# Two 2 MB weight loads of a decoder layer, each cut along the partitions into 120 and 8

## The reference

```python
def peer_ffn(x, w_query, sub_keys, expert_u, expert_v):
    q = (xt @ w_query).reshape(T, PEER_HEADS, 2, PEER_KEY_DIM // 2)
    s = jnp.einsum('thcd,hckd->thck', q, sub_keys)
    s_top, i_top = lax.top_k(s, PEER_TOPK)
    ...                                   # 16 of 256 candidates a head: e_idx, g
    def block(args):
        xb, eb, gb = args
        u = expert_u[eb]
        h = gelu(einsum('td,thkd->thk', xb, u))
        v = expert_v[eb]
        return einsum('thk,thkd->td', gb * h, v)
    ...
```

## Time and profile before

| | |
|---|---|
| median of three runs | 970.4 us (968.57 to 971.49) |
| profiled execution: its own time | 969.14 us |
| its span, first to last instruction | 967.3 us |
| busy: PE / DVE / ACT / POOL | 79% / 61% / 44% / 31% of the span |
| moved by DMA | 335.28 MB, of it 268.45 MB by the gathers (q0) and 66.12 MB by SP (q1) |
| DMA rate from slice 11 of 40 on | 402 to 423 GB/s in each slice but the last |
| chain of waits, by engine | DMA 45%, PE 36%, ACT 8%, DVE 7% |

### The profile page before, as it was taken

How to read it: one execution, slowest core, us unless ns; L and a number is a source line. 1 busy time by engine, 2 the same in 40 slices (tenths; PEclk the granted TensorE clock), 3 DMA queues, 4 the chain that set the end, 5 groups by cost and what they waited for, 6 DMA issues and landing times.

```text
span 967.3 us, 11099 instructions
## 1 busy us (share of the span) xinstructions
PE 766.8 (79%) x3718; PEld 329.6 (34%) x3722; DVE 589.3 (61%) x1409; ACT 428.4 (44%) x1186; POOL 299.7 (31%) x294
## 2 busy tenths in 40 slices
PE   7999999999787999979695757676866666666665
PEld 6876754574443444434131212121211111111010
DVE  1615340453579878877567647587666766767545
ACT  1144212552348967964343424254543434434333
POOL 0010021000325543535333344344443344343320
PEclk9999999999968997979886778597876766677765
DMA  7633233726599999999999999999999999999992
GB/s 262 250 118 121 101 140 142 303 89 249 223 421 421 420 422 405 402 421 420 423 422 421 421 423 421 418 422 421 420 420 421 421 421 421 421 420 421 422 420 110
DMA packets 45353, 335.28 MB, mean 347 GB/s; under 512 B 6000, under 2 KB 6000, under 8 KB 8560
## 3 DMA queue, kind: packets, MB, share of 16 engines
q0 software_dynamic: 36864, 268.45, 67.0%
q1 hardware_dynamic: 8432, 66.12, 17.5%
HBM read 333.50 MB, written 1.05 MB: 346 GB/s over the span
## 4 chain that ended last, share of the span: by engine, by line
DMA 45%; PE 36%; ACT 8%; DVE 7%; issue 3%; POOL 1%; DVEq 0%; SPq 0%; POOLq 0%; ACTq 0%
DMA late<-in_uv,eidx 32%; DMA ring<-in_uv,eidx 11%; PE ps L691 9%; PE ps L1027 7%; PE ps L683 6%; ACT late L1075 4%; ACT L1075 3%; PE ps L815 3%; PE ps L850 3%; DVE late L1731 2%; PE ps L959 1%; DMA wring<-in_wts 1%; DVE ring L1731 1%; ACT tmp L1075 1%; POOL late L1825 1%
## 5 line engine op out<-in xcount | busy, mean ns | idle before, releaser
L1075 ACT ACTIVATE late<-late 128x1 f32<-128x1 f32 (+3 forms) x787 | 221.9, 285 | 345.1 <-DVE late L1731 325.5
L1027 PE MATMUL ps<-ring,late 64*64 64x512 f32 x928 | 161.0, 779 | 95.7 <-ACT late L1075 95.5
L1027 PE MATMUL ps<-late 64*64 64x512 f32 x960 | 169.9, 799 | 65.3 <-ACT late L1075 65.2
L1825 POOL DMA_INDIRECT late<-in_uv,eidx x120 | 134.3, 1119 | 242.4 <-PE ps L1027 177.0
L1731 DVE CUSTOM_DVE_ANT_0 late<-late,x_sb 128x1024 f32<-128x1024 f32 x120 | 146.9, 1225 | 99.2 <-DMA late<-in_uv,eidx 98.6
L1731 DVE CUSTOM_DVE_ANT_0 ring<-ring,x_sb 128x1024 f32<-128x1024 f32 x116 | 142.1, 1225 | 87.2 <-DMA ring<-in_uv,eidx 86.7
L1825 POOL DMA_INDIRECT ring<-in_uv,eidx x116 | 126.8, 1093 | 189.4 <-PE ps L1027 180.8
L1075 ACT ACT_TABLE_LOAD x80 | 102.6, 1283 | 13.3 <-PE ps L683 11.9
L1027 PEld LDWEIGHTS ps<-ring,late 64*64 64x64 f32 x928 | 29.2, 154 | 195.6 <-ACT late L1075 181.4
L1027 PEld LDWEIGHTS ps<-late 64*64 64x64 f32 x960 | 32.1, 161 | 172.3 <-ACT late L1075 154.1
L691 PE MATMUL ps<-wring,tmp 128*128 128x347 f32 (+4 forms) x256 | 85.4, 492 | 0.0
(11 more groups left out here) (235 smaller groups left out, 745.2 us busy)
## 6 DMA issues: line engine op xcount, KB each, us to landing
wring<-in_wts SPq DMA_DIRECT2D x22, 2048.0 KB, 8.7
wring<-in_wts SPq DMA_DIRECT2D x2, 1428.0 KB, 5.8
wring<-in_wts SPq DMA_DIRECT2D x2, 1388.0 KB, 6.3
lnw<-in_ln SPq DMA_DIRECT2D x4, 512.0 KB, 12.5
late<-in_uv,eidx POOLq DMA_INDIRECT x120, 17.5
ring<-in_uv,eidx POOLq DMA_INDIRECT x116, 17.8
wring<-in_wts SPq DMA_DIRECT2D x3, 512.0 KB, 7.4
wring<-in_wts SPq DMA_DIRECT2D x1, 1432.0 KB, 5.8
```

What stands on the lines that cost most here:

```text
L1027: last = mm(o[t][n * HD:(n + 1) * HD, :], factor[tokens, :], values[tokens, n * 512:(n + 1) * 512], start=start, stop=stop, skip_group_che ...
L1075: return nc.scalar.activation(out, in_, func, **kw)
L1825: G.indirect_dma_start(row(slots[g]), None, uv, bass.IndirectOffsetOnAxis(eidx[:, u % 2, k:k + 1], 0)).then_inc(row_here[slots[g]], 16)
```

## The change

Pieces 27 and 28 (`k - len(pieces)` is -2 and -1) are each sent by two DMAs instead of one: partitions 0 to 119 with the piece's old semaphore, and partitions 120 to 127 with a semaphore of their own (`rest_here[0]`, `rest_here[1]`). `next_piece` waits for both.

```diff
+NARROW = (-2, -1)
+MOST = 120
...
+        rest_here = [sem(f"rest_here{n}") for n in range(len(NARROW))]
...
+                elif k - len(pieces) in NARROW:
+                    sp.dma_start(dst[0:MOST], src[0:MOST]).then_inc(w_here[k % WSLOTS], 16)
+                    sp.dma_start(dst[MOST:P], src[MOST:P]).then_inc(rest_here[NARROW.index(k - len(pieces))], 16)
                 else:
                     sp.dma_start(dst, src).then_inc(w_here[k % WSLOTS], 16)
...
                 if k:
                     pe.wait_ge(w_here[k % WSLOTS], 16 * (k // WSLOTS + k % WSLOTS))
+                if k - len(pieces) in NARROW:
+                    pe.wait_ge(rest_here[NARROW.index(k - len(pieces))], 16)
                 return piece_view(k)
```

## The result

The changed kernel takes 988.58 us (median of six runs, 987.86 to 990.0) against 970.75 us (six runs, 968.57 to 973.77) before: 1.0185 times as long, 95% interval 1.0167 to 1.0204. It is slower by 17.8 us, and the forecast of 971.7 us with its range up to 974.3 was wrong.

A forecast was written before the change was run, and what follows sets the result against it. DMA transfers bound the kernel, which ends with the last gather's landing plus 12 us. The last engine gets 1.26 us more, narrow transfers and other edits cost nothing: 970.4 + 1.26 = 971.7 us, range 966.2 to 974.3.

The forecast's parts named there:

- the cost of a transfer of 120 partitions: Pieces 27 and 28 in flight: taken as nothing; upper bound 10.1 us more on 15 engines.
- the narrow transfers are slower in themselves: Rival, 554 to 609 us, all 15 engines: packets take longer, price 5.0 to 10.1 us, 975.4 up to 980.5; chance 0.10.
- What an engine is given or spared there is still in its backlog at 945 us: From 554 and 597 us to the drain: minus 10.1 us on one engine, plus 1.26 us on eight, nothing on seven.
- among the eight: Likeliest case, end of the gathers: the last engine gets extra packets, plus 1.26 us, 971.7 us; chance 0.38.
- spared: Rival, drain after 945 us: the last engine is relieved, gain 2.6 to 3.8 us, middle 967.2 us; chance 0.34.
- untouched: Rival, end of the gathers: the last engine is one of the seven unchanged, 970.4 us; chance 0.18.
- The end is the landing of the last gather and a tail: End of program: last gather lands at 955.24 us, then a tail of fixed length, 12.1 us.
- The time is the time to move the bytes: For two thirds of the span, from slice 11, time is moving bytes at some 421 GB/s.
- SP's extra DMAs and PE's extra wait: At pieces 27 and 28: two more DMAs on SP and one more landing awaited per piece cost nothing.
- PE's cover: Pieces land 66 and 71 us before first use, so a landing later by even 10 us is hidden.
- Two signs of the slower transfers: Under 415 GB/s at share 1.01 between 554 and 610 us, and pieces landing later than 13 us.

The follow-up runs named there:

- Halves: Against the kernel before, pieces 27 and 28 each sent as partitions 0 to 63 and 64 to 127: 985.80 us, ratio 1.0165.
- strips: Against the kernel before, pieces 27 and 28 each sent by eight DMAs of 16 neighbouring partitions: 1001.78 us, ratio 1.0334.
- combs: Against the kernel before, pieces 27 and 28 each sent by eight DMAs of 16 partitions eight apart: 986.49 us, ratio 1.0174.
- the crossed pair: Against the kernel before, eight DMAs a piece: neighbouring partitions written from rows eight apart, 1001.93 us; partitions eight apart written from neighbouring rows, 985.45 us.
- piece 28 alone: Against the kernel before, only piece 28 cut as 120 and 8 partitions, piece 27 in one DMA: 982.53 us, again 981.56 us.

## Why the prediction was wrong

**The step that failed** is the cost of a transfer of 120 partitions: "The nearest row is a piece of 128 partitions in flight beside gathers: 425 GB/s from 600 to 609 us, against 416 without it, so mixing the two costs nothing there. I take nothing". That row was about mixing, not about width. The term that was put at nothing measured 17.7 us of transfer, and 17.8 us of time. Whole pieces of 128 partitions leave the rate at 421 GB/s beside gathers, cut by columns or not; 120 partitions alone bring the stretch down to 354. Halves, strips, combs and the crossed pair show that the rate follows the partitions that are written together: 214 GB/s in the trough of the halves, 156 in that of the strips. That engines hold each other up at a shared way into SBUF, as A has it, is the reading that fits every run, but no row shows which engine wrote where. By the port map of the Trainium skill, "SBUF — State Buffer", cited at the halves, partitions 0 to 63 reach 8 of the 16 ports, and 0 to 15 reach four. The order of the two rates agrees with that.

**The upper bound was too low as well.** The rival *the narrow transfers are slower in themselves* named the place, and a mechanism that fits the runs, with a chance of 0.10 and a price of at most "16 packets x 0.63 = 10.1 us". That is the pieces' own packets at half rate, with the gathers unhindered. The time that the packets of each queue took (q0 the gathers, q1 SP; packets, MB, share of 16 engines' span) parts the two. Kernel before:

```profile
q0 software_dynamic: 36864, 268.45, 67.0%
q1 hardware_dynamic: 8432, 66.12, 17.5%
```

Kernel after:

```profile
q0 software_dynamic: 36864, 268.45, 66.6%
q1 hardware_dynamic: 8446, 66.12, 18.1%
```

SP's packets took 0.181 x 986.1 - 0.175 x 967.3 = 9.2 us more of all 16 engines, which is near the bound. The gathers' packets, the same 36864, took 0.666 x 986.1 - 0.670 x 967.3 = 8.6 us more, which the bound left out. Each of the two is good to about 1 us, as the shares are rounded; the sum is 17.8. So the gathers in flight are held up about as much as the pieces. Whether they wait behind a piece's packet on the same engine or at the way into SBUF itself, no row shows.

**Engines level or not.** "What an engine is given or spared there is still in its backlog at 945 us" is not borne out. That an engine was spared is likely by the packets of q1. A cut into halves has 8464 of them, 16 more for each piece, so a DMA seems to bring one packet for each engine that takes part, beside its data. By that, 120 partitions on 15 engines and 8 on 8 make 135 + 16 = 151 instead of 128 + 16 = 144 a piece, and 14 more for two, which are the 8446 above; where the 8 are left out, 135 a piece give the 8414 that the trace has. An engine 10.1 us ahead would leave the share at 15/16 of 1.01, 0.95, for some 10 us before the drain. With the 8 partitions left out, where one engine is spared and none loaded, the share is 1.00 to 1.02 up to 958 us, and the drain then has its old shape, one engine alone at 0.06. Where the lead went is not shown. In the kernel after the share is 0.94 from 570 to 580 us, but it is 1.07 in the step before, and as packets are counted where they start, this is no sign of an idle engine. Which engine is last stays open. The forecast (*among the eight*), the rival *spared* and the rival *untouched* all turned on it, and together held 0.90 of the chance, over a difference of at most 5 us.

**What held.** The end is the landing of the last gather and a tail: 951.59 + 21.49 = 973.08, and the span of 986.1 leaves 13.0 us behind it (12.1 before). The time is the time to move the bytes, so bytes missing at 560 us come back as time at the end, nearly one to one here (17.7 against 17.8 us) and within 2 us in the other kernels that cut these two pieces, apart from piece 28 alone (9.2 against 11.9, and 8.8 against 11.3). SP's extra DMAs and PE's extra wait cost nothing (the cut by columns). PE's cover held: where the 120 partitions go alone they land after 18.8 us, 7 later than the earlier trace rows, under the 66 us of cover. Two signs of the slower transfers were named beforehand: under 415 GB/s between 554 and 610 us, which the trace of the kernel after shows, and landings over 13 us, which the 18.8 show.

**Why the rival was thought unlikely.** The argument for it (shares that cover other partitions than the gathers' do) was weighed against an even 421 GB/s of transfers that all had 128 partitions. No row that was read from the kernel before could speak against it, so it should have kept a chance near that of the others and a price that includes all traffic in flight.

## What to carry to other kernels

In a stretch bound by transfers, a load cut along the partitions can halve the rate of everything in flight (211 to 226 GB/s instead of 421 here), not of its own bytes alone; cut along the columns instead (no loss here with two DMAs of 128 x 2048). When a resource is new to the trace, price it against all the work that shares it. And a row that holds for one shape is no evidence on another: where no row speaks against a mechanism, keep its chance.

## What was not expected of the hardware

- The same 16 partitions a DMA cost twice as much when neighbouring (30.1 us missing for two pieces) as when eight apart (15.0), and it is the written partitions that decide (crossed: 29.9 and 15.8).
- A DMA of 8 partitions, 1/16 of a piece, cost 1.7 to 2.7 us of a time bound by transfers, where its bytes alone are 0.3 us (0.13 MB at 421 GB/s).
- A wait of PE of 4.9 us at 142 us was followed by a granted clock of 0.50, and the products behind it took 2.4 us more.
- Transfers cut along the partitions slow the gathers beside them as well: the gathers' packets took 8.6 us more of all 16 engines, the pieces' 9.2.
